# A third of the merge gates' projection computed in attention's steps, cache keys and values single-buffered

## The reference

```python
h = _rms_norm(x, norm_mix_pre)
p = h @ w_in                     # 5640 columns
qa, ka, va, qkv_b, z_b, a_b, b_b, gate_a, gate_b = jnp.split(p, split_at, axis=-1)
oa = band attention of qa, ka, va (8 heads of 64; a frame reads its own chunk of 64 and the 8 before;
     a stream reads its 512 cached keys and its own 16), softmax with a bias by relative position
ob = gated delta rule of the convolved qkv_b, with a_b, b_b, z_b
y_a = oa @ w_proj_a
y_b = ob @ w_proj_b
merged = jax.nn.sigmoid(gate_a) * y_a + jax.nn.sigmoid(gate_b) * y_b
x = x + _rms_norm(merged @ w_out, norm_mix_post)
x = x + _rms_norm(jnp.square(jax.nn.relu(_rms_norm(x, norm_mlp_pre) @ w_up)) @ w_down, norm_mlp_post)
```

## Time and profile before

| | us |
|---|---|
| median of 3 runs | 2033.51 |
| lowest, highest | 2029.74, 2036.84 |
| span of the profiled execution | 2028.7 |
| projection products, first to last | about 25 to 594 |
| attention, first to last instruction of PE | 596 to 784 |
| delta rule and tail | 785 to the end |

### The profile page before, as it was taken

The page is one execution under the profiler, slowest core; times in us unless marked ns, Lnnn a source line. Parts: engine busy times, 40 slices in busy tenths (PEclk is TensorE's granted clock), DMA queues, the critical chain, the costliest instruction groups (busy, mean ns, idle before and its releaser), DMA issues. The chain is left out here.

```text
span 2028.7 us, 34282 instructions
## 1 busy us (share of the span) xinstructions
PE 1945.0 (96%) x14050; PEld 1759.9 (87%) x14050; DVE 746.8 (37%) x1482; ACT 634.4 (31%) x1283; POOL 590.6 (29%) x456
## 2 busy tenths in 40 slices
PE   7999999999998888899799999999999999999998
PEld 7899999999994566678699879999999999999997
DVE  5211777111125664565553182222222222222225
ACT  5101222100016664344443245222222222222222
POOL 3111111111132002543354144333333333333333
PEclk9999999999998998999899999999999999999999
DMA  4322223522227213131253232111111111111114
GB/s 119 108 89 88 76 88 118 209 88 88 88 97 238 92 64 84 44 96 39 62 158 105 104 125 88 47 43 42 42 42 42 42 42 42 42 42 42 42 60 169
DMA packets 159273, 169.22 MB, mean 83 GB/s; under 512 B 14187, under 2 KB 130043, under 8 KB 159150
## 3 DMA queue, kind: packets, MB, share of 16 engines
q1 hardware_dynamic: 152814, 141.52, 22.7%
q10 hardware_dynamic: 6336, 25.96, 3.2%
HBM read 126.84 MB, written 40.55 MB: 83 GB/s over the span
## 5 line engine op out<-in xcount | busy, mean ns | idle before, releaser
L2369 DVE TENSOR_TENSOR t_acc<-t_acc,t_B 128x512 f32<-128x512 f32 x252 | 173.3, 688 | 538.6 <-PE t_B L2475 538.6
L116 PE MATMUL i_ps<-x_hi,i_w_lo 128*128 128x384 f32 x1008 | 337.5, 335 | 0.0
L116 PE MATMUL i_ps<-x_hi,i_w_hi 128*128 128x384 f32 x1008 | 337.2, 335 | 0.0
L116 PE MATMUL i_ps<-x_lo,i_w_hi 128*128 128x384 f32 x1008 | 337.2, 335 | 0.0
L2462 PE MATMUL t_B<-t_merged_hi,t_wm_lo 128*128 128x384 f32 x768 | 256.9, 335 | 1.0 <-POOL t_wm_lo L2052 1.0
L2462 PE MATMUL t_B<-t_merged_lo,t_wm_hi 128*128 128x384 f32 x768 | 256.6, 334 | 0.0
L2462 PE MATMUL t_B<-t_merged_hi,t_wm_hi 128*128 128x384 f32 x768 | 256.6, 334 | 0.0
L106 POOL TENSOR_TENSOR i_w_lo<-i_w_raw,i_w_hi 128x1024 fp32r<-128x1024 f32 x44 | 105.4, 2395 | 433.4 <-ACT i_w_hi L101 433.4
L2052 POOL TENSOR_TENSOR t_wm_lo<-t_raw,t_wm_hi 128x1024 fp32r<-128x1024 f32 x49 | 118.8, 2425 | 295.9 <-ACT t_wm_hi L2127 295.9
L116 PEld LDWEIGHTS i_ps<-x_lo,i_w_hi 128*128 128x128 f32 x1008 | 189.8, 188 | 0.0
L116 PEld LDWEIGHTS i_ps<-x_hi,i_w_lo 128*128 128x128 f32 x1008 | 189.7, 188 | 0.0
(11 more groups left out here) (344 smaller groups left out, 3465.9 us busy)
## 6 DMA issues: line engine op xcount, KB each, us to landing
proj<-i_out ACTq DMA_DIRECT2D x44, 576.0 KB, 2.8
i_w_raw<-in_w_in SPq DMA_DIRECT2D x44, 512.0 KB, 3.9
t_raw<-in_w_up SPq DMA_DIRECT2D x32, 512.0 KB, 4.2
t_raw<-in_w_down SPq DMA_DIRECT2D x32, 512.0 KB, 3.6
t_gates<-proj SPq DMA_DIRECT2D x48, 192.0 KB, 2.7
a_k_cache<-in_cache_attn_k SPq DMA_DIRECT2D x8, 1024.0 KB, 6.1
a_v_cache<-in_cache_attn_v SPq DMA_DIRECT2D x8, 1024.0 KB, 5.3
d_c<-proj SPq DMA_DIRECT2D x3, 1536.0 KB, 7.6
```

Of the source, the lines that this page charges most:

```text
L116: last = pe.matmul(out, a[s][:, c, :], b[:, c, tokens], start=k == 0, stop=k == n - 1)
L2369: dve.tensor_tensor(a, a, B[(ND * j + d) % 4][:, :], ALU.add).then_inc(added, 1)
```

## The change

The products of the last third of the tokens (group 2, tokens 768 to 1151) with the 16 gate slabs leave the projection. There PE does two groups for a gate slab, DVE copies two banks, ACT stores 768 columns (`KEPT`). The last group's `x_hi` and `x_lo` get tensors of their own that live on through attention.

In attention each gate slab n takes the four steps st = 4 + 4n to 7 + 4n (parts 0 to 3). At the end of PE's step, behind values and side jobs, stand the products of three chunks (9 matmuls) in parts 0 and 1, of two chunks (6) in part 2, none in part 3, all into a new PSUM bank GP. DVE copies the bank at the end of its part-2 step (`gate_out`), SP stores it. The weights are loaded a second time: SP loads slab n+1 at its place for part 0 of slab n, ahead of which stands a wait for POOL's low part of slab n (one raw buffer); ACT makes the high part of slab n+1 in two halves at the end of its part-2 and part-3 steps (slab 0 at steps 1 and 2), waiting for the load; POOL makes the low part in one instruction, behind all else on its list; PE's part 0 waits for it. For slab 1 ACT waits besides until the kept keys, values and conv rows are saved.

To make room, cached keys and values and the turned keys have one buffer instead of two, the scores have three banks instead of four (for five key blocks the two units of a pair share the middle one, and the parts are issued in another order with one wait between), and `c0` is loaded at the end of attention.

```diff
+KEPT = T - TG
@@ stage_in_proj: ACT, DVE, PE of the gate slabs
+            def store_gates(i, s):
+                act.dma_start(env.proj[bass.ds((2 * i + s) * P, P), 0:KEPT], st[s][:, 0:KEPT]).then_inc(sent[s], 16)
-            plain(NZ // 2 + 2, HALF)
+            plain(GATES_AT, HALF, NTG - 1)
+            slabs(1, GATES_AT, NTG)
+            slabs(GATES_AT, HALF, NTG - 1)
@@ stage_attention: memory
-        kc = [sb(f"k_cache{i}", [P, 4, AW]) for i in range(2)]
-        vc = [sb(f"v_cache{i}", [P, 4, AW]) for i in range(2)]
-        kt = [sb(f"k_cache_t{i}", [P, 4, REACH]) for i in range(2)]
+        kc, vc = sb("k_cache", [P, 4, AW]), sb("v_cache", [P, 4, AW])
+        kt = sb("k_cache_t", [P, 4, REACH])
-        S = [c.enter_context(nc.psum_tensor(f"a_S{i}", [P, 1024], F32)) for i in range(2)]
+        SB = c.enter_context(nc.psum_tensor("a_S", [P, 1536], F32))
+        NGATE, GSTEPS, GSTART = NSLAB[1], 4, 4
+        def gate_part(st):
+
+            n = st - GSTART
+            return divmod(n, GSTEPS) if 0 <= n < NGATE * GSTEPS else (None, None)
@@ SP
             def load_k(b):
-                if b >= 2:
-                    sp.wait_ge(tk_made, side["K", 4 * (b - 2) + 3] + 1)
+                if b:
+                    sp.wait_ge(tk_made, side["K", 4 * (b - 1) + 3] + 1)
+            def load_gate_w(n):
+                if n:
+                    sp.wait_ge(w_lo_made, n)
+                sp.dma_start(w_raw[:, :, :], w_in[:, :, COL_GATE + n * P:COL_GATE + (n + 1) * P]).then_inc(w_landed, 16)
+            load_k(0)
+            load_v(0)
             sp.wait_ge(pre_d, (NPRE) // 2)
             sp.wait_ge(pre_a, (NPRE + 1) // 2)
+            load_gate_w(0)
+            for st in range(STEPS):
+                n, part_ = gate_part(st)
+                if part_ == 0 and n + 1 < NGATE:
+                    load_gate_w(n + 1)
+                if part_ == 2 and n:
+                    store_gate(n - 1)
+                b, h = divmod(st, STEP)
+                if h == 7 and b + 1 < NB:
+                    load_k(b + 1)
+                if h == 5 and 0 < b < NB:
+                    load_v(b)
+            store_gate(NGATE - 1)
+            sp.wait_ge(g_prod, NGATE)
@@ POOL, behind bias_s
+            for n in range(NGATE):
+                pool.wait_ge(w_hi_made, 2 * n + 2)
+                pool.tensor_tensor(w_lo[n % 2][:, :, :], w_raw[:, :, :], w_hi[n % 2][:, :, :].bitcast(F32), ALU.subtract
+                                   ).then_inc(w_lo_made, 1)
@@ ACT
+            def gate_high(n, half):
+                act.wait_ge(w_landed, 16 * n + 16)
+                if n >= 2:
+                    act.wait_ge(g_prod, n - 1)
+                if n == 1:
+                    act.wait_ge(saved, 16 * 6)
+                cs = slice(4 * half, 4 * half + 4)
+                act.activation(w_hi[n % 2][:, cs, :], w_raw[:, cs, :], ACT.Copy).then_inc(w_hi_made, 1)
                 for j in side_jobs(st):
                     side_out(j)
+                if st in (1, 2):
+                    gate_high(0, st - 1)
+                n, part_ = gate_part(st)
+                if part_ in (2, 3) and n + 1 < NGATE:
+                    gate_high(n + 1, part_ - 2)
@@ DVE
+            def gate_out(n):
+                dve.wait_ge(g_prod, n + 1)
+                if n == 0:
+                    dve.wait_ge(saved, 16 * 6)
+                if n >= 2:
+                    dve.wait_ge(g_sent[n % 2], 16 * (n // 2))
+                dve.tensor_copy(g_out[n % 2][:, :], GP[:, 0:TG]).then_inc(g_free, 1)
@@ PE: scores of a pair
+                parts = ((0, 0, W), (1, 0, W)) if n < 5 else ((e, 512, W), (1 - e, P, W), (e, 0, 512), (1 - e, 0, P))
+                for j, (i, a, z) in enumerate(parts):
+                    half = slice(AD * i, AD * i + AD)
+                    if j == 3:
+                        pe.wait_ge(far_scores, (b - 4) * (AH // 2) + h // 2 + 1)
@@ PE: the gates
+            def gates(n, cc):
+
+                if cc == 0:
+                    pe.wait_ge(w_lo_made, n + 1)
+                    if n:
+                        pe.wait_ge(g_free, n)
+                h, lo, xh, xl = w_hi[n % 2], w_lo[n % 2], env.x_hi[NTG - 1], env.x_lo[NTG - 1]
+                for a, b in ((lo, xh), (h, xl), (h, xh)):
+                    last = pe.matmul(GP[:, 0:TG], a[:, cc, :], b[:, cc, :],
+                                     start=cc == 0 and a is lo, stop=cc == DC - 1 and a is h and b is xh)
+                if cc == DC - 1:
+                    last.then_inc(g_prod, 1)
                 for j in side_jobs(st):
                     side_turn(j)
+                if n is not None:
+                    for cc in range(3 * part_, min(3 * part_ + 3, DC)):
+                        gates(n, cc)
```

More of the change, by code:

```diff
@@ L115, in slab_products @@
         for a, b in ((w.lo, x_hi), (w.hi, x_lo), (w.hi, x_hi)):
-            last = pe.matmul(out, a[s][:, c, :], b[:, c, tokens], start=k == 0, stop=k == n - 1)
+            last = pe.matmul(out, a[s][:, c, :], b[:, c, :], start=k == 0, stop=k == n - 1)
             k += 1
@@ L290, in products @@
                 for cc in range(part * DC // 2, (part + 1) * DC // 2):
-                    for a, b in ((w.lo, env.x_hi), (w.hi, env.x_lo), (w.hi, env.x_hi)):
-                        last = pe.matmul(env.ps[NTG * sl + g][:, 0:TG], a[sl][:, cc, :], b[:, cc, tokens],
-                                         start=cc == 0 and a is w.lo, stop=cc == DC - 1 and a is w.hi and b is env.x_hi)
+                    for a, b in ((w.lo, env.x_hi[g]), (w.hi, env.x_lo[g]), (w.hi, env.x_hi[g])):
+                        last = pe.matmul(env.ps[NTG * sl + g][:, 0:TG], a[sl][:, cc, :], b[:, cc, :],
+                                         start=cc == 0 and a is w.lo, stop=cc == DC - 1 and a is w.hi and b is env.x_hi[g])
                 if part == 1:
@@ L358, in stage_in_proj, with counts @@
         HALF = NS // 2
+        GATES_AT = NSLAB[0] // 2
         CREDIT = env.credit
+        def counts(g, groups):
+            return NTG - g if g == groups - 1 else 1
         @block.sync
@@ L427, in _ @@
                     store(act, i, s)
-            plain(NZ // 2 + 2, HALF - 1)
+            with act.Fori(GATES_AT, HALF - 1) as i:
+                for s in range(2):
+                    split_hi(act, w, i + 1, s)
+                    evacuated(i, s)
+                    store_gates(i, s)
             for s in range(2):
                 evacuated(HALF - 1, s)
-                store(act, HALF - 1, s)
+                store_gates(HALF - 1, s)
             act.wait_ge(env.v_in, 16)
@@ L478, in plain @@
                         dve.wait_ge(sent[s], 16 * i + 16)
-                        for g in range(NTG):
+                        for g in range(groups):
                             m = 3 * (2 * i + s) + g
@@ L559, in _, with slabs @@
             last.then_inc(ab_made, 1)
[L560 to L568, removed]
+            def slabs(a, b, groups):
+                with pe.Fori(a, b) as i:
+                    for s in range(2):
+                        pe.wait_ge(w.lo_made, 2 * i + s + 1 + WRING)
+                        for g in range(groups):
+                            m = 3 * (2 * i + s) + g
+                            pe.wait_ge(free, m + 1)
+                            last = slab_products(pe, w, s, env.x_hi[g], env.x_lo[g], ps[3 * s + g][:, 0:TG], range(DC))
+                            last.then_inc(prod, counts(g, groups))
+            slabs(1, GATES_AT, NTG)
+            slabs(GATES_AT, HALF, NTG - 1)
 def stage_attention(env):
@@ L723, in _ @@
                     "(c p) t -> p c t", p=P)).then_inc(env.c_in, 16)
-            for b in range(2, NB):
-                load_k(b)
-                load_v(b)
             sp.wait_ge(saved, 16 * 6)
+            for n in range(2):
+                sp.wait_ge(g_sent[n], 16 * len(range(n, NGATE, 2)))
             sp.wait_ge(env.c_in, 32)
@@ L833, in side_out @@
                     b, pair = divmod(x, 4)
-                    if b >= 2:
-                        act.wait_ge(s_made, stream(b - 2) + 1)
-                    act.activation(kt[b % 2][:, pair, :], TK[:, :], ACT.Copy).then_inc(tk_read, 1)
+                    if b:
+                        act.wait_ge(s_made, stream(b - 1) + 1)
+                    act.activation(kt[:, pair, :], TK[:, :], ACT.Copy).then_inc(tk_read, 1)
             for st in range(STEPS):
@@ L887, in soft @@
                     b = u // STEP
+                    cached, own = stream_scores(u)
                     if b == 0:
```

114 lines of the change are left out of this document (69 added, 45 removed).

## The result

The changed kernel takes 2063.74 us (median of 4 runs, 2062.09 to 2066.74) against 2033.22 (4 runs): ratio 1.0152, 95% interval 1.0136 to 1.0168. It is slower by 30.5 us; forecast were 2069 and a range of 2036 to 2096. The profiled execution has a span of 2060.5 us, 31.8 more than before.

The account below looks back on a forecast made before the run. TensorE (PE), busy 96% of the span, was taken as the bound. Attention +104.5 and projection -66.5 gave net +38 us on the median 2033.51, rounded down by 2: 2069 us, range 2036 to 2096 (own range 2052 to 2092).

Parts of the forecast that it names:

- (c): Attention, slabs 1 to 15: PE waits for POOL's low part at each slab's first block, +25 us (bounds 0 and +35).
- Rival 1: Attention: ACT catches up, the low part comes in time from slab 1; (c) and (g) fall away, 2045 us; 15%.
- (d): Attention's start: PE waits for slab 0's low part, behind POOL's earlier work, 7.7 us, taken as +8 (5 to 11).
- before 560: Sign against the forecast: POOL's first subtraction in attention ends before 560 us.
- (a): Attention: 384 products add 66.5 us of PE work, and the ends of 48 blocks +4 us.
- (b): Attention: blocks fill ten of PE's 14 holes between an even step's end and the odd step's transposes, -8 us.
- (e): Attention's start: after the 8 us wait PE's clock starts low again, +3 us (-3 to +5).
- rival 3: Attention: seven waits of 2 us and more each bring half clock, some 5 us each: +35, 2104 us; 8%.
- Half speed beyond the start: Sign against the forecast: the profile's clock row shows PE at half speed beyond attention's start.
- (f): Attention's five-block scores in three shared banks: unequal neighbours hold each other up, +4 us (0 to +7).
- (g): Attention: POOL's 16 subtractions hold up VectorE beside them, some 0.6 us each; +2 us (0 to +5).
- (h): Attention's other edits (single cache buffers, SP's queue, weight and conv loads, copies, ACT's halves, gate stores) hidden, costing nothing.

Follow-up runs that it names:

- early: The changed kernel with ScalarE's two halves of a slab's high part one step earlier each (parts 1 and 2): 2033.36 us, ratio 1.0013 to the kernel before.
- halves: The changed kernel with POOL's low part made in two halves, PE waiting for each separately, ACT's work left late: 2030.10 us, ratio 0.9992 to the kernel before.
- start8: The changed kernel with the gate slabs at steps 8 to 71 instead of 4 to 67: 2060.86 us, ratio 1.0148 to the kernel before.
- early8: The changed kernel with the edits of both early and start8: 2028.82 us, ratio 0.9989 to the kernel before.
- products_alone: no_gates plus the 384 products in their places, with ready operands and no waits: 2016.68 us, ratio 0.9927 to the kernel before.
- no_gates: The changed kernel without any gate work in attention (no load, split, product, copy or store): 1968.78 us, ratio 0.9694 to the kernel before.
- unread2: The changed kernel with all gate work, but its products take ready operands and don't wait for the low part: 2023.54 us, ratio 0.9946 to the kernel before.
- late: The changed kernel with both halves of a slab's high part made in part 3: 2077.54 us, ratio 1.0198 to the kernel before.

## Why the prediction was right, and where it was not

**What leaves the projection**: -66.5 forecast, -65.4 measured.

**(c) The waits for the low part**, the step that decides. For slabs 1 to 15 the forecast was 0.2, 2.3, 2.7, 2.0, 1.3, 2.2, 2.4, 1.9, 0, 1.6, 1.5, 2.7, 1.7, 0.7, 2.0, together 25.2; the profile after has 0.83, 2.20, 2.61, 1.99, 1.45, 2.13, 2.28, 1.65, 0, 1.23, 1.54, 2.61, 1.66, 0.76, 2.12, together 25.1. One of the two longest and the shortest but for slab 9, slabs 12 and 14:

```profile
738.26 0.44 PE L1162 MATMUL a_GP<-x_hi,a_gate_w_lo 128*128 128x384 f32 x1 [2.61 <-POOL a_gate_w_lo L858]
...
772.56 0.44 PE L1162 MATMUL a_GP<-x_hi,a_gate_w_lo 128*128 128x384 f32 x1 [0.76 <-POOL a_gate_w_lo L858]
```

Setting ACT's end of one step against PE's end of the next, in the trace of the kernel before, was enough. I take it that ACT and PE keep their distance because both go by the same transposes; that reason is argued, not tested. Rival 1, that ACT would catch up, was wrong in the changed kernel. early and halves show that the *cause* was named rightly: make the chain shorter at either link, and the waits of slabs 1 to 15 are gone or nearly so (0.6 us left in early, none in halves).

**(d) The first slab**: 7.7 forecast, 5.4 measured. POOL was as late as forecast:

```profile
551.14 1.12 PE L1124 MATMUL a_TK<-ident,a_k_cache 128*128 128x128 f32 x4 [0.39 <-ACT a_k_cache_t L914]
...
554.82 0.50 POOL L855 COPY a_bias_s<-a_bias_s 128x384 f32<-128x384 f32 x1
555.29 2.34 POOL L858 TENSOR_TENSOR a_gate_w_lo<-a_gate_w,a_gate_w_hi 128x1024 fp32r<-128x1024 f32 x1
557.68 0.69 PE L1162 MATMUL a_GP<-x_hi,a_gate_w_lo 128*128 128x384 f32 x1 [5.42 <-POOL a_gate_w_lo L858]
```

The subtraction ended at 557.6, where "557" had been said; the sign "before 560" in the same sentence of the prediction contradicted its own 557, and came true without the forecast being wrong. PE came later to it, because ACT had waited 1.7 us for the first weights, ahead of the transposes' copies; that wait was said to be hidden under the other, and it was. What the first wait is worth depends on the rest. start8 takes it away and wins 3 us at most, as one of 2.3 us comes at step 68 and the slow start gets longer; between early and early8, where no other wait for a low part is left, the same shift brings 8.1 us of steps and 4.5 us of time.

**(a) and (b) The products and the holes**: +70.5 and -8 forecast. The blocks' ends, +4, cost nothing (products_alone: 66 us for 384 products), and the idle time that products can fill from the step ends was 10.6 us there (27.9 - 14.5, less 2.8 for the key wait of no_gates). In the changed kernel the idle time outside the new waits fell by 6.4 us (30.5 - 24.1).

**(e) The clock, and rival 3**: +3 forecast, 10 measured, and not where it was forecast. Taking the products' 66 us and the 5 us that the kernel before loses itself, 226.0 - (149.8 - 5.2) - 66 = 15.4 us of PE's busy time is owed to the lower level, 10 more than before. The five later stretches, 20 us at half speed, make up those 10; the start, for which the +3 stood, lost about 5 as before. So a form of rival 3, given 8%, came true beside the likeliest case: the clock fell behind five waits of 2.0 to 2.6 us, and not behind two others of 2.1, and each fall cost some 2 us, not 5. "Half speed beyond the start" had been named as a sign that the forecast is wrong; it came, and on the clock the forecast was wrong. The argument against it, a stretch of 3.85 busy us in 5 with the clock at 1.00, was too weak: idle time spread over many small holes isn't one wait. The Trainium skill (TensorE: Matmul & The Clock Gate, What's actually happening) has the array at 1.2 GHz after idle time; the trace agrees behind the five waits and not behind the two others.

**(f) The scores' order**: +4 forecast, 0 measured. A five-block pair of the changed kernel:

```profile
789.53 1.35 PE L1078 MATMUL a_S<-k,q 64*128 64x128 f32 x8
790.82 0.77 PE L1109 MATMUL a_TR<-ident,a_s 128*128 128x128 f32 x5
```

1.35 us, and 1.29 to the next instruction, the same as in the old order. The +7 that was derived from the Trainium skill's sentence on program order (TensorE: Matmul & The Clock Gate, Part 3, The mechanism) doesn't come about in this order of sizes; the measurement decides.

**(g) VectorE beside POOL**: +2 forecast. The hold is real and longer than thought (up to 2.1 us more for one scaling, where some 0.6 had been taken), but it costs PE next to nothing here (0.4 us from the first stream's turn on in unread2). The Trainium skill (GPSIMD Engine Reference, 1. Specifications) names the shared interface, and the rows of the scaling and the subtraction agree with it.

**(h) Edits at nothing**: nearly right; no_gates measured 2.4 us for them. The cached keys' load was said to have 13 us of cover, by the mean step of 2.68 us. The steps before the second stream's keys are needed take 1.4 us each in no_gates ((563.3 - 546.6) / 12), and PE waited 2.8 us for them there; in the changed kernel products and waits cover it. That a step of up to 3.3 us is less than the chain of 3.1, in (c), was a slip without effect.

**The sum** was +104.5 for the steps and is +100.3: 66 products, 10 clock, 24 idle (30.5 of new waits less some 6 of old ones). Too high were the blocks' ends by 4.5, the scores' order by 4 and the first wait by 2.6; the clock was too low by 7; the holes and VectorE's term together were right, -6 forecast and -6.4 measured. That errors of 11 and 7 us nearly cancel is luck, as far as the total goes; the 25 us that decide the sign are not. The last 2.8 us, behind attention, were not forecast. The code there is the same in all thirteen profiled executions, and that stretch takes 1241.7 to 1248.6 us in them, so this is within their spread.

## What to carry to other kernels

Work moved from a dense stage into the gaps of another brings its own chain of producers with it: before moving it, set the end of the last producer's step in the trace against the point at which the consumer will ask, step by step, and start the chain a whole step earlier where they come close. Where PE takes its work in order, a wait of 2 us costs those 2 us and then, at times, some 2 more at half clock, so the same amount of work was worth +30 us or -11 (unread2) by nothing but whether PE waited for the operands. Put the block where the engine itself waits, which may be in the middle of a step, and not only at its end.

## What the runs showed of the hardware

- TensorE's clock fell to half behind some single waits of 2.0 to 2.6 us (1.8 to 3.1 in `late`) in a stage in which it was 82% busy, and 6.5 us more of waits in `late` took the mean from 0.94 to 0.89. With no such waits, in products_alone, it stayed at 1.00 for 225 us, with 14.5 us of idle time spread over holes of at most 1.2 us.
- A scaling or copy of VectorE from SBUF to SBUF ended only after POOL's two-operand subtraction beside it: 2.62 us for 0.5, a pair of copies 2.28 for 0.4. Beside POOL's halves of 1.3 us it was 1.56. POOL took 2.34 us, and 2.57 where VectorE's scaling had started first. VectorE's reads of PSUM with a bias from SBUF weren't held: 0.82 us for 128x640 beside a subtraction, and without one (changed kernel):

```profile
672.99 0.82 DVE L967 CUSTOM_DVE_ANT_0 a_s<-a_S,a_bias 128x640 f32<-128x640 f32 x1 [1.18 <-PE a_S L1078]
...
715.65 0.82 DVE L967 CUSTOM_DVE_ANT_0 a_s<-a_S,a_bias 128x640 f32<-128x640 f32 x1
```

- Score matmuls of two row groups with unequal sizes side by side (128 and 512 columns) took no longer than equal ones: 1.35 us for eight records.
